# Latent scores from split halves, one more square added by GpSimd, and a modulation product moved by one panel

## What is computed

```
def mla_mixer(hx, hc, w_down, q_norm, kv_norm, w_uq, w_ukv, w_o, cos, sin, ctx_out):
    ...
        d = h @ w_down
        cq = rms_norm(d[..., :MLA_Q_RANK], q_norm)
        ckv = rms_norm(d[..., MLA_Q_RANK:MLA_Q_RANK + MLA_KV_RANK], kv_norm)
    ...
        q = (cq @ w_uq).reshape(B, N, H, MLA_NOPE + MLA_ROPE).transpose(0, 2, 1, 3)
        kv = (ckv @ w_ukv).reshape(B, N, H, MLA_NOPE + MLA_V).transpose(0, 2, 1, 3)
    ...
        s = jnp.einsum('bhqd,bhkd->bhqk', qn, kn) + jnp.einsum('bhqr,bkr->bhqk', qr, kr)
```

## Time and profile before

| | |
|---|---|
| median of 3 runs | 2290.31 us |
| profiled execution | 2288.82 us |
| its span, first to last instruction | 2287.0 us |
| TensorE (PE) busy | 2267.6 us, 99% |
| weight loads (PEld) | 2014.3 us, 88% |
| DVE busy | 1697.3 us, 74% |
| ACT busy | 950.1 us, 42% |
| GpSimd (POOL) busy | 122.9 us, 5% |
| mean granted TensorE clock | 0.999 |

### The profile page before, as it was taken

How to read it: one execution, slowest core, us unless ns; L and a number is a source line. 1 busy time by engine, 2 the same in 40 slices (tenths; PEclk the granted TensorE clock), 3 DMA queues, 4 the chain that set the end, 5 groups by cost and what they waited for, 6 DMA issues and landing times.

```text
span 2287.0 us, 35250 instructions
## 1 busy us (share of the span) xinstructions
PE 2267.6 (99%) x14406; PEld 2014.3 (88%) x14406; DVE 1697.3 (74%) x2772; ACT 950.1 (42%) x1414; POOL 122.9 (5%) x85
## 2 busy tenths in 40 slices
PE   9999999999999999999999999999999999999998
PEld 9899999899998888898789888888888888989997
DVE  7989889989889858754546983884884673797775
ACT  6766645766542122235553212223321222475443
POOL 0110010200100000010001000001000001001001
PEclk9999999999999999999999999999999999999999
DMA  7355475355545545532111553553454453304543
GB/s 281 132 193 187 163 253 193 123 191 192 193 147 208 182 147 187 183 111 83 43 69 56 204 197 105 184 180 115 157 193 157 138 180 102 135 37 148 184 154 124
DMA packets 67025, 355.08 MB, mean 155 GB/s; under 512 B 7344, under 2 KB 10544, under 8 KB 43056
## 3 DMA queue, kind: packets, MB, share of 16 engines
q1 hardware_dynamic: 66304, 352.49, 44.4%
q10 hardware_dynamic: 560, 0.33, 0.0%
HBM read 351.75 MB, written 1.05 MB: 154 GB/s over the span
## 4 chain that ended last, share of the span: by engine, by line
PE 91%; DVE 6%; ACT 2%; issue 0%; DMA 0%; DVEq 0%; ACTq 0%
PE bank L567 90%; DVE sb_w_lo L2271 2%; ACT sb_w_hi L1498 1%; PE bank L1450 1%; DVE sb_products L2305 1%; PE bank L1324 0%; ACT sb_nP L1498 0%; DVE sb_products_up L2323 0%; DMA sb_res<-x 0%; DVE sb_decays L3014 0%; DVE sb_mid L2912 0%; ACT sb_decays L1498 0%; DVE sb_nP L3002 0%; DVE sb_mid L2883 0%; DVE sb_latP L3139 0%
## 5 line engine op out<-in xcount | busy, mean ns | idle before, releaser
L1498 ACT ACTIVATE sb_w_hi<-sb_raw 128x2048 fp32r<-128x2048 f32 (+5 forms) x301 | 491.3, 1634 | 395.6 <-PE bank L567 388.7
L2271 DVE TENSOR_TENSOR sb_w_lo<-sb_raw,sb_w_hi 128x2048 fp32r<-128x2048 f32 (+3 forms) x280 | 563.9, 2014 | 117.5 <-ACT sb_w_hi L1498 112.7
L567 PE MATMUL bank<-sb_f_pair,sb_w_hi 128*128 128x256 f32 (+1 forms) x2090 | 522.6, 339 | 1.5 <-DVE sb_w_lo L2271 1.2
L567 PE MATMUL bank<-sb_h_hi,sb_w_hi 128*128 128x512 f32 (+1 forms) x1400 | 510.8, 365 | 0.6 <-DVE sb_w_lo L2271 0.4
L567 PE MATMUL bank<-sb_h_lo,sb_w_hi 128*128 128x512 f32 (+1 forms) x1400 | 507.3, 362 | 0.0
L567 PE MATMUL bank<-sb_h_hi,sb_w_lo 128*128 128x512 f32 (+1 forms) x1400 | 507.2, 362 | 0.0
L567 PEld LDWEIGHTS bank<-sb_f_pair,sb_w_hi 128*128 128x128 f32 x2090 | 360.2, 190 | 46.5 <-DVE sb_w_lo L2271 3.5
L2305 DVE CUSTOM_DVE_ANT_0 sb_products<-sb_raw,sb_cond,sb_params 128x1024 f32<-128x1024 f32 x276 | 354.8, 1285 | 32.1 <-DVEq L2307 16.2
L567 PE MATMUL bank<-sb_f_pair,sb_w_lo 128*128 128x256 f32 (+1 forms) x1122 | 365.9, 326 | 0.0
L567 PEld LDWEIGHTS bank<-sb_h_hi,sb_w_hi 128*128 128x128 f32 x1400 | 264.1, 189 | 43.0 <-issue 0.9
L567 PEld LDWEIGHTS bank<-sb_h_lo,sb_w_hi 128*128 128x128 f32 x1400 | 264.2, 189 | 41.2 <-issue 0.5
(11 more groups left out here) (330 smaller groups left out, 2926.9 us busy)
## 6 DMA issues: line engine op xcount, KB each, us to landing
sb_raw<-w_mod SPq DMA_DIRECT2D x144, 512.0 KB, 3.2
sb_raw<-w_l_up SPq DMA_DIRECT2D x44, 1024.0 KB, 4.8
sb_raw<-w_l_in SPq DMA_DIRECT2D x22, 1024.0 KB, 6.8
sb_raw<-w_l_down SPq DMA_DIRECT2D x32, 704.0 KB, 4.7
sb_raw<-w_m0a_up SPq DMA_DIRECT2D x22, 1024.0 KB, 4.8
sb_raw<-w_m0b_up SPq DMA_DIRECT2D x22, 1024.0 KB, 4.8
sb_raw<-w_m1a_up SPq DMA_DIRECT2D x22, 1024.0 KB, 4.8
sb_raw<-w_m1b_up SPq DMA_DIRECT2D x22, 1024.0 KB, 4.8
```

The costliest lines, as they stand in the source:

```text
L567: return nc.tensor.matmul(out, lhsT, rhs, start=start, stop=stop, skip_group_check=True)
L1498: return nc.scalar.activation(out, in_, func, **kw)
L2271: V.tensor_tensor(split_part(*at, w_lo[s]), landed_part(*at, raw[raw_slot(*at)]), split_part(*at, w_hi[s]).bitcast(F32), ALU.subtract).the ...
```

## The change

Three things are changed.

1. **Latent scores.** The plain queries and keys of a pair are kept as high and low halves (`q_hi`, `q_lo`, `k_hi`, `k_lo`), and a unit's plain score is one `mm3` per head. ACT's copy out of PSUM now writes the high half; DVE makes the low half from the PSUM bank and the high half (`pair_low`, 16 in all), so that the bank stays taken until then. The tiles of a pair come in the order 2, 0, 3, 1, 4, 5, 6. The new tiles lie over constants and parameters that only the first block reads, and over `sq`; tables are reordered and padded for it, and the rotations use `rstd` as work space in place of `sq`.
2. **Squares.** Where a norm goes by stream, GpSimd adds x's tile 6 too (a sixth addition, 256 wide), `sums(0)` has two products in place of three, and stands after step k = 2 at all four places.
3. **Modulation.** In `l0_up` and `l1_up` the chunk is loaded one panel later, and go 1 moves from the head of tile 9 to its end, behind the low half of panel 11 and the taps of tile 9.

```diff
+PAIR_TILES = (2, 0, 3, 1, 4, 5, 6)
...
-_mods = {SPLIT_AT[at] + 2: chunks for at, chunks in MOD_STEPS.items()}
+_mods = {SPLIT_AT[at] + (3 if at[0] in FF1_UP else 2): chunks for at, chunks in MOD_STEPS.items()}
...
-BY_STREAM = (KD + 2, KD - 3, 0, 2 * T)
+BORDER_ADDS = KD - 2
+BY_STREAM = (KD + 2, [(k, k + 1, 0, 2 * T) for k in range(1, KD - 2)] + [(KD - 2, KD - 1, 0, T)])
...
+        for i, (q_hi, k_hi) in enumerate(((sq_at, second_consts), (params_at, second_consts + 4096))):
+            slot = M + 4 * (7 * 512 + 3840 * i)
+            pair_q.append((score_tile(f"q_hi{i}", q_hi), score_tile(f"q_lo{i}", slot)))
+            pair_k.append((score_tile(f"k_hi{i}", k_hi), score_tile(f"k_lo{i}", slot + 4 * 1792)))
...
-                    pe.wait_ge(S("sq_added"), a + KD - 3)
+                    pe.wait_ge(S("sq_added"), a + BORDER_ADDS)
                     pe.wait_ge(S("norm_sq"), b + KD + 2 * s)
                     mm(bank[7][:, at], inv[1024][:, :], sq_sum[:, at], True, False)
-                    mm(bank[7][:, at], inv[1024][:, :], sq[:, 0, at], False, False)
+                    if s:
+                        mm(bank[7][:, at], inv[1024][:, :], sq[:, 0, at], False, False)
...
-                                if s == 1 and t == 0 and k == 4:
+                                if s == 1 and t == 0 and k == 2:
                                     sums(0)
...
-                        if m == KD - 2 and k == 3:
+                        if m == KD - 2 and k == 2:
                             sums(0)
...
             def tile_free(p, t):
-                if 7 * p + t >= 2:
-                    pe.wait_ge(S("pair_evac"), 7 * p + t - 1)
-                if p >= 2 and t == 1:
+                if pair_count(p, t) > 2:
+                    pe.wait_ge(S("pair_evac"), pair_count(p, t) - 2)
+                if t in (1, 5, 6) or (p and t == 2):
+                    pe.wait_ge(S("pair_low"), 4 * p + {2: 0, 1: 1, 5: 2, 6: 3}[t])
+                if p >= 2 and t == 0:
                     pe.wait_ge(S("pair_rope"), p)
...
-                for t in range(2):
-                    pair_tile(p, t, w, 2, t * T, 4).then_inc(S("pair_tile"), 1)
+                for t in PAIR_TILES[0:4]:
+                    if t < 2:
+                        last = pair_tile(p, t, w, 2, t * T, 4)
...
                 if b == 0:
                     pe.wait_ge(S("pair_rope"), p + 1)
+                    pe.wait_ge(S("pair_low"), 4 * p + 4)
                 for h2 in range(2):
-                    mm(bank[h2][:, 0:W], qn[:, h2, q], kn[:, h2, 2 * T - W:2 * T], True, False)
+                    mm3(bank[h2][:, 0:W], both(pair_q[p % 2], slice(None), h2, q),
+                        both(pair_k[p % 2], slice(None), h2, slice(2 * T - W, 2 * T)), True, False)
...
-                    if (name + "_up", n - 1) in IN_TWO_GOES:
-                        mod_part(name + "_up", n - 1, 1, products_up)
                     ahead()
...
-                    if (name + "_up", n) in IN_TWO_GOES:
-                        mod_part(name + "_up", n, 0, products_up)
+                    for at in (n, n - 1):
+                        if (name + "_up", at) in IN_TWO_GOES:
+                            mod_part(name + "_up", at, n - at, products_up)
...
+            def pair_low(p, *tiles):
+
+                for t in tiles:
+                    dve.wait_ge(S("pair_evac"), pair_count(p, t))
+                    hi, lo = (pair_q if t > 3 else pair_k)[p % 2]
+                    at = t % 4
+                    V.tensor_tensor(lo[:, at, :], pair_bank(p, t)[:, :], hi[:, at, :].bitcast(F32),
+                                    ALU.subtract).then_inc(S("pair_low"), 1)
+
...
             low("mla_pair0", 0)
+            pair_low(0, 0, 1)
             for k in range(4):
                 latent_split(k, "q_high", k, "q_low")
...
             low("mla_pair1", 1)
+            pair_low(0, 4, 5)
+            pair_low(1, 0, 1)
             pair_rope(0)
             low("mla_pair1", 0)
             lat_max(0)
+            pair_low(1, 4)
             lat_max(1)
             lat_probs(0)
+            pair_low(1, 5)
...
+                if u in (4, 8):
+                    pair_low(u // 4 + 1, 0, 1, 4, 5)
```

More of the change, by code:

```diff
@@ L158, in whole_norm @@
 def whole_norm(tiles, a=0, b=T):
-    return tiles, tiles - 2, a, b
-BY_STREAM = (KD + 2, KD - 3, 0, 2 * T)
+    return tiles, [(k, k + 1, a, b) for k in range(1, tiles - 1)]
+BORDER_ADDS = KD - 2
+BY_STREAM = (KD + 2, [(k, k + 1, 0, 2 * T) for k in range(1, KD - 2)] + [(KD - 2, KD - 1, 0, T)])
+assert len(BY_STREAM[1]) == BORDER_ADDS
 NORMS = (([whole_norm(KD), whole_norm(4), whole_norm(KD)] * LAYERS)[1:] + [whole_norm(KD, T, 2 * T), whole_norm(KD, 0, 2 * T)]
@@ L180 @@
         ("ffn_conv", FF1_TILES * 8))]
-    + [("final1", KD), ("cond", KD * 2), ("mod_norm", LAYERS * 3 * KD), ("mod_b", LAYERS * N_MOD * KD),
+    + [("spare", 52), ("final1", KD), ("cond", KD * 2), ("mod_norm", LAYERS * 3 * KD), ("mod_b", LAYERS * N_MOD * KD),
        ("final2", KD), ("q_norm", 4), ("kv_norm", 2), ("sink", SWA_HEADS)])
-CONSTS, CONST_W = table([("ident", P), ("tri", 2 * T), ("rot", P), ("cos1", T), ("sin1", T), ("cos2", T), ("sin2", T),
-                         ("causal", 2 * T), ("decay_mask", 384), ("cmp_add", 32), ("cmp_keep", 32),
-                         ("window", 2 * T), ("fold", 2)])
+CONSTS, CONST_W = table([("ident", P), ("rot", P), ("cos2", T), ("sin2", T), ("window", 2 * T),
+                         ("tri", 2 * T), ("cos1", T), ("sin1", T), ("causal", 2 * T), ("decay_mask", 384),
+                         ("cmp_add", 32), ("cmp_keep", 32), ("spare", 64), ("fold", 2)])
+FIRST_BLOCK_CONSTS = CONSTS["tri"][0]
+assert CONSTS["fold"][0] - FIRST_BLOCK_CONSTS == 2 * 1024 and PARAMS["final1"][0] == 1024
 class Tally:
@@ L414, in latent_low, with pair_count @@
             return lat_lo[k // 3][:, k % 3, :]
+        def pair_count(p, t):
+            return 7 * p + PAIR_TILES.index(t) + 1
         def pair_bank(p, t):
-            return bank[2 + (7 * p + t) % 2]
+            return bank[2 + (pair_count(p, t) - 1) % 2]
         def rot_bank(p):
@@ L546, in _ @@
             squares_at, added = 0, 0
-            for i, (squares, adds, a, b) in enumerate(NORMS):
-                for k in range(1, adds + 1):
-                    pool.wait_ge(S("norm_sq"), squares_at + k + 1)
+            for i, (squares, adds) in enumerate(NORMS):
+                for k, need, a, b in adds:
+                    pool.wait_ge(S("norm_sq"), squares_at + need)
                     if added:
@@ L677, in norm_by_stream @@
                 b = take("norm_sq", KD + 2)
-                a = take("sq_added", KD - 3)
+                a = take("sq_added", BORDER_ADDS)
                 c = take("rms_done", 2)
@@ L1262, in pair_tile @@
                 for k in range(K):
-                    if p == 0 and t in (0, 4):
-                        pe.wait_ge(S("q_low" if t else "kv_low"), k + 1)
+                    if p == 0 and t == 4:
+                        pe.wait_ge(S("q_low"), k + 1)
                     last = mm(o, cols(w, at0 + k * P)[0], latent_low(src + k), False, k == K - 1)
@@ L1296, in pair_rot @@
             def pair_rot(p):
-                _, qr, _, _, _ = pairs[p % 2]
+                qr, _, _ = pairs[p % 2]
                 pe.wait_ge(S("pair_evac"), 7 * p + 7)
@@ L1302, in lat_scores @@
                 p, b, q, W = lat_unit(u)
-                qn, qr, qrot, kn, _ = pairs[p % 2]
+                qr, qrot, _ = pairs[p % 2]
                 if u:
@@ L1329, in lat_products @@
                 p, b, _, W = lat_unit(u)
-                vv, nk = pairs[p % 2][4], W // P
+                vv, nk = pairs[p % 2][2], W // P
                 if u >= 2:
@@ L2141, in pair_evac @@
                     run(dst[t], src, ACT.Copy).then_inc(S("pair_evac"), 1)
-                    if t == 3 and p < 3:
+                    if t == PAIR_TILES[3] and p < 3:
                         high(f"mla_pair{p + 1}", 1)
@@ L2170, in lat_high @@
                     ACT.Copy).then_inc(S("lat_high"), 1)
-            pair_evac(0, range(7))
-            pair_evac(1, range(4))
+            pair_evac(0, PAIR_TILES)
+            pair_evac(1, PAIR_TILES[0:4])
             lat_exps(0)
@@ L2187, in _ @@
                     lat_exps(u + 2)
-                    pair_evac(u // 4 + 1, range(7))
+                    pair_evac(u // 4 + 1, PAIR_TILES)
                 if u in (9, 10):
@@ L3127, in pair_rope @@
             def pair_rope(p):
-                qn, qr, qrot, kn, vv = pairs[p % 2]
+                qr, qrot, _ = pairs[p % 2]
                 dve.wait_ge(S("pair_rot"), p + 1)
                 rope(qrot.unsqueeze(1), qr[:, 0:T].unsqueeze(1), rot_bank(p)[:, 0:T].unsqueeze(1), con("cos2"),
-                     con("sin2"), 1, "pair_rope", sq)
+                     con("sin2"), 1, "pair_rope", rope_work)
             def lat_max(u):
```

53 lines of the change are left out of this document (31 added, 22 removed).

## The result

The changed kernel takes 2293.13 us (median of 22 runs, 2291.45 to 2294.56), the kernel before beside it 2289.99 (22 runs, 2288.96 to 2290.59): a ratio of 1.0014 with a 95% interval of 1.0008 to 1.0020. That is 3.1 us longer, 0.14%. The interval leaves out 1, so the lengthening is clear of the noise, but it lies within the 0.2% that the prediction calls no change. Its profiled execution took 2294.05 us, 5.2 more than that of before.

The account below looks back on a forecast made before the run. TensorE was taken to bound the kernel, with 91% of the chain. Latent attention +2.9, squares -0.6 and modulation -1.3 made 1.0 us longer, 2291.3 us; own range 2288.5 to 2294.5, range for all 2288.0 to 2295.5.

Parts of the forecast that it names:

- Scores: the gain: Latent attention: fp32r score products save TensorE 0.32 per wide unit and 0.12 per narrow one, 3.5 us less.
- Query latents: Pair 0's tile 4 is held 1.5 us because the query latents' low halves come later in DVE's list.
- Tile 6: Pair 0's tile 6 waits 1.7 us for tile 4's low half, behind a rotation and a panel's low half.
- Scores 0: First scores wait 2.8 us for pair 0's rotation, now behind the low half of pair 1's tile 1.
- Tile 1: A pair's tile 1 waits for tile 0's bank: 0.13 in each of three pairs, 0.4 us together.
- The sum of the latent attention: Stalls of 6.4 less 3.5 gained: the latent attention gets 2.9 us longer.
- Pairs 2 and 3 have no such stalls: Latent attention, later pairs: low halves are asked for one unit before the next softmax needs DVE, so no such stalls.
- The clock's rival: Clock falls in the new stall before scores 0, costing 2.6 to 5.3 us: 2295.5 us, chance 0.10.
- Squares: Norms by stream: 0.9 won in three down projections, 0.3 lost at the output projection, together 0.6 us less.
- Modulation: Up projections: panel 11's wait of 0.97 goes, panel 12 waits 0.3; 1.3 us less in two layers.
- The low halves hold nobody up: Rival: DVE's new low halves cost TensorE no waits in latent attention; 5.4 shorter, 2284.9 us, chance 0.07.
- Only the latent attention shows: Rival: gains at modulation and squares are lost to neighbouring waits; 2.9 longer, 2293.2 us, chance 0.18.

Follow-up runs that it names:

- run 6: Changed kernel, DVE's list reordered against the stalls, mla_pair1 0's low half moved ahead, output-projection sums back behind k = 4: 2285.42 us, ratio 0.9979.
- run 5: Changed kernel with pair 0's rotation also moved behind the low half of mla_pair1 0, lengthening the stall before scores 0: 2294.92 us, ratio 1.0022.
- run 7: Kernel before with only the squares and modulation parts of the change, latent attention as it was: 2288.73 us, ratio 0.9993.
- run 4: Changed kernel with six idle float32 products on TensorE ahead of the wait of scores 0, DVE's order kept: 2292.24 us, ratio 1.0008.

## Why the prediction was right, and where it was not

The forecast was 2291.3, no change that can be told; the time is 2293.1, inside its own range and not to be told from no change by the bound set. The steps, in the order of the prediction:

- *Scores: the gain* was right for a unit. Scores 1 take 2.56 in place of 2.87. From one unit's transposes to the next, where no new wait stands between, a wide unit gains 0.33 and 0.34 and a narrow one 0.14 and 0.15 (forecast 0.32 and 0.12). The sum of 3.5 is not reached, even without the three stalls (1.5 in run 6).
- *Query latents* 1.5: measured 1.57 (4.32 less 2.75). *Tile 6* 1.7: 1.68 (it was due at 1071.00 and began at 1072.68). *Scores 0* 2.8: 2.86 (due 1081.58). All three by the mechanism named: DVE's strict list.
- *Tile 1* was mis-sized: 0.31 in place of 0.13 each (in pair 2 it was due at 1125.77 with a first product of 0.23, and came at 1126.01 with one of 0.30).
- *The sum of the latent attention*, 2.9, is the step that failed: the profile has 6.24. 1.55 of it is the clock, which the sum held at 1.00. The other 1.8 are small terms. Up to the first transposes the prediction's own terms give 5.5 (0.13 + 1.5 + 1.7 + 2.8 less 0.64; the 5.7 that it states does not agree with its sum), and 7.62 less the clock's 1.55 is 6.07: 0.6 more, of which tile 1 of pair 0 is 0.18 and the three stalls 0.1. Behind that, 2.6 was to come back (it states some 2.5) and 1.38 did, although the scores of a unit gained what they should. Tile 1 costs 0.18 more in each of two pairs. The stretch from the transposes of units 4 and 8 to the next pair's tiles takes 4.57 in place of 4.37, where 0.12 was to be won. And TensorE waits 0.8 for DVE's maxima where it waited 0.3. "Pairs 2 and 3 have no such stalls" was right of the three stalls, not of small waits.
- *The clock's rival* had too small a chance with 0.10: the clock fell in the profiled execution and, as inferred above, in about half of all. The price was lower than given, 1.55 against 2.6 to 5.3. The rows left it open, and the text leaned on the wait of about a microsecond as the nearer one. It also misread the other: it took the 0.54 at the end for the work of some 6 us without products, but there the clock fell at about 2280.5, while the last products still ran, behind waits of 0.68 and 0.55. The trace now has a wait of 1.5 (before tile 6) with no fall and 2.7 with one. The Trainium skill ("TensorE: Matmul & The Clock Gate", section on HAM oscillation), cited there, has next work start cold after a long enough gap. The trace agrees that the stall is paid beyond its own length, and after 4.38 us (run 5) the first work read 0.52; but after 2.70 us the first microsecond of work still ran at 1.00, and the extra was 1.55, not the stall over again.
- *Squares*, -0.6: -0.58 in the trace, by other shares. The three down projections gave 0.14 to 0.18 each and not 0.3, and the output projection gained 0.11 where 0.3 was to be lost. So that the sum fits is luck. The wait of 1.01 for GpSimd came as worked out (forecast 1.0).
- *Modulation*, -1.3: -1.0. Panel 12's wait is 0.45 and 0.44, not 0.3. Its low half was over when forecast (209.36 less the start's 0.44 is 208.92, forecast 208.9); TensorE came to it 0.2 earlier.
- *The other rivals.* "The low halves hold nobody up" fell with the three stalls. Run 6, without them, comes near its time (2285.42 against 2284.9) but not its sum: in the trace the stages gain some 3.0 (latent attention 1.5, up projections 1.0, norms 0.5) where it had 5.4. "Only the latent attention shows" has the measured time (2293.2) but not the mechanism: run 7 shows both small gains.

In short: the median missed the forecast lengthening of 1.0 by 2.1. The terms make more: about 0.85 for the clock (half of 1.7, if it falls in half of the executions), 1.8 of small terms in the latent attention and 0.3 of the modulation, 2.95 together. The 0.8 between is of the size by which start and last layer vary; no run shows that it lies there. That the time stayed inside the range of 2288.5 to 2294.5 is in part luck: the stage on which the forecast turned came out at over twice its size, and the longer half's median (2294.05) is 0.45 from the upper end.

## What to carry to other kernels

When work moves from a fast engine to one with time to spare, write out that engine's list and ask of each new entry who stands behind it: here the engine was idle more than half of the time, its order cost 6.1 us at three places, and moving three low halves (run 6) made a slower kernel a faster one (2293.1 to 2285.4, of which some 0.9, by the profiles, lies in the last layer and is not theirs). Price a new wait of TensorE with the clock behind it and not only with its length, and look for it in a narrow window, since a mean of 0.998 hides it. If the order can't be mended, idle products in the wait can hold the clock: in run 4 they won 0.9 of the median.

## What the runs showed of the hardware that was not expected

- The times of one program, with the same wait of 2.7 us, form two groups of 11 executions, 1.7 us apart. The mean clocks, 0.998 and 0.999, suggest that the granted clock falls in the longer group and not in the other; only one execution, of the longer, was profiled. Behind the same last products of the span the fall comes between 0.2 us before and 2.1 us after the last product's end, over nine profiled executions.
- A wait of 4.38 cost hardly more clock than one of 2.70: the mark grew by 1.65, the wait by 1.68.
- Code that no edit touches, from the last down projection's sums to the last product, took 325.96 us in the profiled execution before, 326.16 after, and 325.18 to 326.99 in the others. TensorE's wait for the first panel is up to 1.8, but the same product behind the start (the first sums of squares) stands between 108.18 and 108.91, so that the start varies by 0.7. A part worth half a microsecond can be read stage by stage in the trace, but hardly in the totals.
